# Moving the indexer's dots behind their rope, turning the attention outputs and moving the pool tiles in a two-layer decoder step

## What is computed

```python
dots = jnp.einsum('bqhd,bld->bqhl', qi, ki) * (IDX_DIM ** -0.5)
s = jnp.einsum('bqhl,bqh->bql', jax.nn.relu(dots), wi) * (N_IDX_HEADS ** -0.5)
_, sel = lax.top_k(s, topk)
p = jax.nn.softmax(where(valid, q @ k_sel, -inf)); o = p @ v_sel
out = jnp.einsum('btgc,gcd->btgd', window_mean(xp) - xp, w_pool) * pool_scale
```

## Time and profile before

| | |
|---|---|
| time, median of 3 runs | 1589.93 us (1585.71 to 1590.79) |
| profiled execution: its time, its span | 1585.85 us, 1584.1 us |
| busy: PE, DVE, ACT, POOL | 1435.0, 803.7, 432.3, 184.1 us |
| mean granted clock of TensorE | 0.932 |
| layer 1: third indexer query tile begins | 852.0 us |
| page products end | 907.0 us |
| unit loop begins | 989.5 us |
| output projection begins | 1106.5 us |
| layer 0: the same four | 75.2, 132.0, 214.6, 331.7 us |

### The profile page before, as it was taken

How to read it: one execution, slowest core, us unless ns; L and a number is a source line. 1 busy time by engine, 2 the same in 40 slices (tenths; PEclk the granted TensorE clock), 3 DMA queues, 4 the chain that set the end, 5 groups by cost and what they waited for, 6 DMA issues and landing times. The chain is left out here.

```text
span 1584.1 us, 25392 instructions
## 1 busy us (share of the span) xinstructions
PE 1435.0 (91%) x9676; PEld 1239.6 (78%) x9676; DVE 803.7 (51%) x1752; ACT 432.3 (27%) x761; POOL 184.1 (12%) x200
## 2 busy tenths in 40 slices
PE   4999957998899999999988988599979999999995
PEld 2765643687899999999957547356969999999995
DVE  1127777434665656712142486863366565665221
ACT  3111113534322222422131120254342222224220
POOL 1000354002100000000040005430030000000002
PEclk8999976898999999999979999587989999999997
DMA  8870112002122222222159402020212222222321
GB/s 322 176 103 27 34 36 77 5 28 80 67 93 89 85 91 93 86 97 88 69 215 172 87 1 70 1 81 1 80 41 94 93 87 87 91 103 74 111 76 54
DMA packets 46316, 133.17 MB, mean 84 GB/s; under 512 B 6319, under 2 KB 25615, under 8 KB 38911
## 3 DMA queue, kind: packets, MB, share of 16 engines
q1 hardware_dynamic: 43423, 119.52, 25.2%
q0 software_dynamic: 2816, 12.62, 2.3%
HBM read 119.94 MB, written 12.82 MB: 84 GB/s over the span
## 5 line engine op out<-in xcount | busy, mean ns | idle before, releaser
L779 PE MATMUL ps<-moR_r,W_r 128*128 128x260 f32 x1408 | 285.4, 284 | 0.0
L779 PEld LDWEIGHTS ps<-moR_r,W_r 128*128 128x128 f32 x1408 | 218.1, 190 | 0.0
L779 PE MATMUL ps<-hT_r,QZC_r 128*128 128x260 f32 x896 | 183.4, 286 | 0.0
L779 PE MATMUL ps<-moR_r,QZC_r 128*128 128x260 f32 x704 | 146.5, 289 | 12.3 <-DVE hT_r L1822 12.1
L779 PE MATMUL ps<-moR_r,SQ_r 128*128 128x260 f32 x704 | 142.1, 283 | 0.0
L779 PEld LDWEIGHTS ps<-hT_r,QZC_r 128*128 128x128 f32 x896 | 141.3, 193 | 0.0
L779 PE MATMUL ps<-hT_r,SQ_r 128*128 128x260 f32 x704 | 140.6, 281 | 0.0
L766 PE MATMUL ps<-hT,W 128*128 128x260 f32 x576 | 132.8, 388 | 0.0
L779 PEld LDWEIGHTS ps<-moR_r,QZC_r 128*128 128x128 f32 x704 | 110.6, 192 | 16.0 <-issue 8.6
L766 PEld LDWEIGHTS ps<-hT,W 128*128 128x128 f32 x576 | 109.4, 192 | 17.1 <-issue 0.6
L1864 DVE TENSOR_TENSOR SEL<-ps,rstd 128x520 f32<-128x520 f32 x44 | 30.8, 700 | 154.3 <-PE ps L779 149.4
(11 more groups left out here) (318 smaller groups left out, 2728.0 us busy)
## 6 DMA issues: line engine op xcount, KB each, us to landing
W<-in_w_gates SPq DMA_DIRECT2D x44, 512.0 KB, 3.2
W<-in_w_vals SPq DMA_DIRECT2D x44, 512.0 KB, 3.2
W<-in_w_downs SPq DMA_DIRECT2D x16, 1408.0 KB, 6.0
W<-in_w_pairs SPq DMA_DIRECT2D x12, 1024.0 KB, 7.5
pages_by_slot<-moR SPq DMA_DIRECT2D x8, 1024.0 KB, 5.4
yR<-pages_by_slot SPq DMA_DIRECT2D x16, 512.0 KB, 17.9
W<-in_w_outs SPq DMA_DIRECT2D x8, 1024.0 KB, 4.9
W<-in_w_kv SPq DMA_DIRECT2D x2, 1312.0 KB, 10.3
```

The source lines that it names most:

```text
L779: last = mm(ps[:, 2 * (g % 2) + f, 0:HT], w(k), x(k)[:, f * HT:(f + 1) * HT], start=(k == 0 and n == 0), stop=(k == nk - 1 and n == 2))
```

## The change

Dots are ordered by head pair, then token tile, and stand between the k steps of the tiles that follow the pair's rope (six dots a tile, in the last two indexer query tiles and XP 0 and 1). The search's counts stand between the k steps of XP 2, 3 and the query tiles; ranks follow every other step. Probabilities stay unscaled; `values` takes them as the stationary side (128 columns) and the value rows as the moving side (64), so that queries lie on partitions, and once a token tile VectorE scales its 8 units by the reciprocal sums and TensorE turns the result back. Pool tiles go to unit 24 behind `sample_max`, with their scaling on VectorE; the sample's steps move to earlier units.

```diff
-SCORED = 10
-ROPES = {16: (4,), 18: (5,), 19: (6,)}
+DOTS = [(t, h) for j in range(4) for t in (1, 2, 3) for h in (2 * j, 2 * j + 1)]
+ROPES = {12: (4,), 15: (5,), 17: (6,)}
...
+        ON = SQ[:, 3, 0:SEQ]
-        att = sb("att", [P, 4, 4])
+        att = sb("att", [P, 4])
+        sums = sb("sums", [P, 2, N_HEADS])
...
-                    if extras and k % 4 == 3:
+                    if extras and k in at:
                         extras.pop(0)()
...
+                def dot(d):
+                    def go():
+                        t, h = DOTS[d]
+                        if d == 0:
+                            pe.wait_ge(*kt_ev(l, 4))
+                        if d % 6 == 0:
+                            wait_alone(pe, *rope_done(l, d // 6 + 1))
+                        if d >= 2:
+                            wait_alone(pe, *dot_relu(l, d - 1))
+                        rows = slice(64 * (h % 2), 64 * (h % 2) + 64)
+                        mm(ps[:, 4 + d % 2, 0:P * (t + 1)], qiT[rows, h // 2, t * P:(t + 1) * P],
+                           kiT[rows, 0:P * (t + 1)], start=True, stop=True).then_inc(dot_mm.sem, 1)
+                    return go
...
-                    tile8(QI_T + j, 1 + j // 2, j % 2)
+                    tile8(QI_T + j, 1 + j // 2, j % 2, extras=dots, at=range(2, KD) if j >= 2 else ())
...
+                tile8(XP_T, 3, 0, extras=dots, at=range(2, KD))
                 pe.wait_ge(*rope_done(l, 4))
...
+                tile8(XP_T + 1, 3, 1, extras=dots, at=range(1, KD - 1))
...
+                steps = [scores_by_page] + [count(s) for s in range(COUNTS)] + [pick_a, pick_b, pick_c]
+                page_products()
+                arrived(l, 4)
+                for j in (2, 3):
+                    pe.wait_ge(*evac(l, XP_T + j - 1))
+                    tile8(XP_T + j, 4, j % 2, extras=steps, at=(1, 4, 7) if j == 2 else (1, 3, 5, 7))
...
-                    tile8(Q_T + j, 5 + j // 2, j % 2, extras=counts)
+                    tile8(Q_T + j, 5 + j // 2, j % 2, extras=steps, at=(1, 4, 7))
...
-                    wait_alone(pe, *list_ev(l, 1))
-                    pe.wait_ge(*o_ev(l, 1))
+                    wait_alone(pe, *ss_ready(l, 1))
+                    pe.wait_ge(*qs_ev(l, 2))
+                    pe.wait_ge(*o_ev(l, 2))
...
-                picks = {6: pick_d, 14: pool_tiles, 26: sample_scores, 28: scores_by_row, 33: sample_probs_turned,
-                         34: sample_values}
-                picks.update({21 + q: (lambda q=q: keys_turned(q)) for q in range(4)})
+                def outputs_turned(t):
+                    wait_alone(pe, *o_normed(l, t + 1))
+                    for j in range(4):
+                        last = turn(ps[:, 6 + t % 2, j * P:(j + 1) * P], ON[:, j * P:(j + 1) * P], ident)
+                    last.then_inc(o_turned.sem, 1)
+                picks = {5: pick_d, 21: sample_scores, 23: scores_by_row, 24: pool_tiles, 28: sample_probs_turned,
+                         30: sample_values}
+                picks.update({17 + q: (lambda q=q: keys_turned(q)) for q in range(4)})
+                turned = {8 * t + 12: t for t in range(NT - 1)}
...
-                    pe.wait_ge(*prob_ready(l, i + 1))
+                    pe.wait_ge(*exp_done(l, i + 1))
...
-                        last = mm(ps[64 * n:64 * n + 64, 6 + t % 2, j * P:(j + 1) * P],
-                                  NAT[:, kt, 200 + 64 * n:264 + 64 * n], ART[:, i % 2, kt * P:(kt + 1) * P],
-                                  start=(kt == 0), stop=(kt == t))
+                        last = mm(ps[:, 6 + t % 2, 64 * p:64 * p + 64], ART[:, i % 2, kt * P:(kt + 1) * P],
+                                  NAT[:, kt, 200 + 64 * n:264 + 64 * n], start=(kt == 0), stop=(kt == t))
...
+                    elif steps:
+                        steps.pop(0)()
+                    if i in turned:
+                        outputs_turned(turned[i])
...
+                outputs_turned(NT - 1)
...
+                for ropes, first in (((0,), 0), ((1,), 6), ((2, 3), 12)):
+                    for j in ropes:
+                        rope(j)
+                    for d in range(first, first + 6):
+                        add_dots(d)
...
                 for n, step in enumerate(steps):
                     step()
+                    rank(n % 2)
                     for j in ROPES.get(n, ()):
                         rope(j)
-                rank(4)
-                rope(7)
+                    if n == 18:
+                        rank(3)
+                        rope(7)
...
-                picks = {0: slots, 1: hot_high, 2: hot_low, 3: hot_rows, 9: pick_e, 30: sample_max, 32: sample_probs}
+                picks = {0: slots, 1: hot_high, 2: hot_low, 3: hot_rows, 7: pick_e, 26: sample_probs}
...
-                def normalised(i):
-                    n = P * (1 + i // N_HEADS)
-                    dve.wait_ge(*exp_done(l, i + 1))
-                    then_wait(nc.vector.reciprocal(att[:, i % 4, 2:3], att[:, i % 4, 1:2]))
-                    ts(ARP[i % 4][:, 0:n], ARP[i % 4][:, 0:n], att[:, i % 4, 2:3], None, ALU.mult
-                       ).then_inc(prob_ready.sem, 1)
+                def outputs_normed(t):
+                    dve.wait_ge(*pv_mm(l, N_HEADS * (t + 1)))
+                    if t:
+                        dve.wait_ge(*o_turned(l, t))
+                    nc.vector.reciprocal(sums[:, t % 2, :], sums[:, t % 2, :]).then_inc(o_recip.sem, 1)
+                    wait_alone(dve, *o_recip(l, t + 1))
+                    tt(ON.rearrange("p (h d) -> p h d", h=N_HEADS),
+                       ps[:, 6 + t % 2, :].rearrange("p (h d) -> p h d", h=N_HEADS),
+                       sums[:, t % 2, :].unsqueeze(2).broadcast_to([P, N_HEADS, HD]), ALU.mult).then_inc(o_normed.sem, 1)
+                def pool_out():
+                    for g in range(4):
+                        dve.wait_ge(*tile_done(l, PM_T + g + 1))
+                        ts(hT[:, 4 + g, 0:SEQ], ps[:, 3 + 4 * (g % 2), :], vecs[:, l, 32 + g:33 + g], None, ALU.mult
+                           ).then_inc(pm_ev.sem, 1)
...
+                for i in range(UNITS):
+                    if 3 <= i < 24:
+                        rank(-(-len(ranks) // (24 - i)))
...
+                    masked(i)
+                    if i == 24:
+                        sample_max()
+                        pool_out()
...
+                    if i in (11, 19, 27):
+                        outputs_normed(i // 8 - 1)
...
+                outputs_normed(NT - 1)
```

More of the change, by code:

```diff
@@ L331, in count_bank @@
         def count_bank(s):
-            return (6 if s < 23 - SCORED else 4) + s % 2
+            return 4 + s % 2
         def halves(ap):
@@ L758, in arrived, with product @@
                 pe.wait_ge(*w_in_slot[c % 2](l, 16 * dmas_before(c)))
-            def product(g, lhsT, rhs, nk, extras=None, before=None):
+            def product(g, lhsT, rhs, nk, extras=None, at=(), before=None):
                 for k in range(nk):
@@ L821, in partner @@
                     last.then_inc(rot_mm.sem, 1)
+                def dot(d):
[11 more added lines that the diff above has]
+                    return go
+                dots = [dot(d) for d in range(24)]
                 for j in range(4):
@@ L1219, in layer, with relu @@
                 copy(kT[:, SEQ:TOK], ps[:, 7, 8:8 + NB]).then_inc(kt_ev.sem, 1)
-                q_copy(2, QI_T + 2)
-                q_copy(3, QI_T + 3)
+                def relu(d):
+                    t, h = DOTS[d]
+                    n = P * (t + 1)
+                    act.wait_ge(*dot_mm(l, d + 1))
+                    if d >= 4:
+                        act.wait_ge(*dot_acc(l, d - 3))
+                    nc.scalar.activation(RB[:, d % 4, 0:n], ps[:, 4 + d % 2, 0:n], ACT.Relu).then_inc(dot_relu.sem, 1)
+                for j in range(2):
+                    for d in range(6 * j, 6 * j + 6):
+                        relu(d)
+                    q_copy(2 + j, QI_T + 2 + j)
+                for d in range(12, 18):
+                    relu(d)
                 def xp_copy(j):
@@ L1524, in rope @@
                     tt(dst, TS[:, :], QC[:, j % 2, :], ALU.add).then_inc(rope_done.sem, 1)
-                for j in range(4):
-                    rope(j)
                 def best(t, r):
@@ L1582, in layer @@
                 ts(spread, const("spread"), wcol[:, 8:9], None, ALU.mult).then_inc(w_spread.sem, 2)
+                for d in range(18, 24):
+                    add_dots(d)
                 dve.wait_ge(*sdot_mm(l, 1))
@@ L1587, in layer @@
                 nc.vector.tensor_reduce(snew[:, :], sdot[:, :], AX.X, ALU.add).then_inc(snew_ready.sem, 1)
-                for d in range(8):
-                    add_dots(d)
                 for r in range(TOPK_P // 8):
@@ L1758, in masked @@
                     nc.vector.tensor_tensor_reduce(ARS[:, i % 2, 0:n], ps[:, i % 3, 0:n], out, -1.0, -TAKEN,
[L1759 to L1766 removed]
```

(8 more changed lines are left out.)

159 lines of the change are left out of this document (67 added, 92 removed).

## The result

The changed kernel takes **1625.97 us** (median of 4 runs, 1621.16 to 1629.73), the kernel before beside it 1590.36: a ratio of 1.023 (95% interval 1.019 to 1.027), 35.6 us slower. The prediction had 12.6 us slower and a range that ended at 1616. The side was right; the size was a third of what came.

What follows compares the result with a forecast made beforehand. VectorE was taken to bound only the top-k ranking beside attention units 0 to 14, with TensorE busy elsewhere. Terms 18.8 - 21.5 - 11.9 + 20.9 gave +6.3 us a layer, +12.6 for two: 1602.5 us, range 1580 to 1616.

Steps and rivals of the forecast that it cites:

- A: Third indexer query tile to end of page products, dots moved in behind the rope: +18.8 us a layer.
- B: End of page products to start of unit loop, search beside XP 2, 3 and query tiles: -21.5 us a layer.
- so waits of some 2 us: Search stage before the unit loop: TensorE waits some 2 us for VectorE's search steps of 2.50 us each.
- C: Start of unit loop to unit 16's scores, with fewer ranks and no normalisations: -11.9 us a layer.
- some 8 is only that the pool tiles have left: Units 0 to 15: some 8 of the 11.9 us gained comes from pool tiles leaving, having stood in VectorE's shadow.
- D: Unit 16's scores to the output projection: 8.7 - 0.8 + 1.8 + 1.2 + 4 + 6 = +20.9 us a layer.
- gather wait: Near unit 17: TensorE arrives near 1038.7, the last gather lands at 1042.7: +4 us a layer.
- wait for the maximum: Unit 24: TensorE idles 2.6 us for the mask and sample_max before the pool tiles, part of their +8.7 us.
- the clock term: From unit 16: TensorE at 1.2 GHz until about unit 20, +6 us a layer, ends 0 and 11.
- Rival 2: Value products at half price, 0.13 us each: 0 us a layer, 1590 us; chance 0.12.
- Rival 3: Low clock up to the pool tiles and again at the end: +12.3 us a layer, 1614.5 us; chance 0.20.
- Rival 1: Clock holds at 2.4 GHz from unit 16 through the sample's scores: -4.2 us a layer, 1581.5 us; chance 0.20.

Runs made afterwards that it cites:

- x11_steps_back: The changed kernel with pool tiles at unit 14 (ScalarE scaling) and the sample's steps in their old units; moved dots and new outputs stay: 1599.47 us, ratio 1.006.
- x13_keys_early: The kernel before with only the turns of the gathered keys moved from unit 21 to unit 17: 1610.65 us, ratio 1.015.
- x10_early: The kernel before with only the sample's steps moved to the changed kernel's units, four to six earlier; pool tiles stay at 14: 1625.61 us, ratio 1.024.
- x7_newvalues: The kernel before with the new outputs alone (64 value columns moving, probabilities unscaled, outputs scaled and turned a token tile at a time): 1597.41 us, ratio 1.003.
- x1_pool16: The changed kernel with pool tiles at unit 16 in place of 24, scaled by ScalarE again: 1616.98 us, ratio 1.019.
- x3_narrow: The changed kernel with 32 added products of 8 columns in unit 17, ahead of the wait for gathered keys: 1649.15 us, ratio 1.037.
- x2_wide: The changed kernel with four added products of 128x512 in unit 17, ahead of the wait for gathered keys, results unread: 1614.53 us, ratio 1.018.

## Why the prediction was wrong, step by step

- **A** (+18.8 predicted; +16.4 and +18.2): right. Dots and their k steps take what the rows of before said.
- **B** (-21.5; -17.8 and -16.3): the step that failed is "so waits of some 2 us". TensorE waits 4.7 and 6.0 us for the search. Its own work is 54.6 and 54.8 us busy (2 more than the 52.5 of the sum), and the waits behind the last query tile, 5.7 and 5.4 us, are under the 6.5 given. VectorE's 2.50 us a step held only where no rank (some 3.0 us with one) and no GpSimd operation stood in it.
- **C** (-11.9; -11.7 and -11.8): right as a sum, but not in the split "some 8 is only that the pool tiles have left": with them at unit 14 again, x11_steps_back has C at 51.7, so their leaving is worth 4.5.
- **D** (+20.9; +27.1 and +29.5): gather wait (3.0 and 4.2), wait for the maximum (2.7), end (1.2) and values (0.235 us a product at 2.4 GHz; predicted 0.24) came as priced. Rival 2 is out. (The estimate of 0.21 us worked out from the Trainium skill, TensorE: Matmul & The Clock Gate, section LDWEIGHTS, is 0.025 below the measured product.) The step that failed, and the larger of the two, is the clock term, +6 with "The drop behind sample_scores costs about what it did (0)". The +6 and the gather's 4 were about right for what they cover: x13_keys_early, which has just these two in the kernel before, with its old value products, measured 8.8 and 11.5. The return came in layer 0 at unit 21, 15.8 us behind the first key turn (forecast: 13.3, unit 20), just ahead of the sample's scores, and in layer 1 not before them. But the drop behind the scores was priced at nothing though the change moved it among other units and gave these other products. It lasted until the pool tiles ended it, 14.7 us and about half of their own 6.3 (0.73) in layer 0 and all of 1079 to 1106 in layer 1. The drop behind the sample's values lasted to the end in layer 0 (0.50) and for most of what was left in layer 1 (0.63).
- **Rival 3** (low clock up to the pool tiles and again at the end, +12.3 a layer, chance 0.20) is what happened, up to its price: with B's 3.7 and 5.2 us on top its 1614.5 would have been 1623.4. Its argument against, "it needs a low stretch longer than any in the trace beside full work", was no argument: no stretch of before had these products in it. Rival 1 is out: units 16 to 23 never ran at 1.00, but for the scores of unit 21 in layer 0.

## What to carry to other kernels

When a step is moved, price again what follows it in its new place, the clock above all: a drop that lasted 12 us behind the same 16 products lasted 29 behind them five units earlier (x10_early), and 44, up to the end of the loop, when the value products that follow took 64 moving and 128 stationary columns in place of 128 and 64 (x7_newvalues). A busy TensorE is not always a TensorE at 2.4 GHz (61.4 of 62.6 us busy at 0.50 in x1_pool16); in a stage where it is the bound, look up in the trace what TensorE does behind each drop, and whether the change puts other work there. And move a consumer of a gather forward only as far as the gather lands: here, in x13_keys_early, a wait of 2.6 us came with 9 to 12 us more in the stage.

## What was not expected of the hardware

- TensorE stayed at 1.2 GHz for 62.6 us while busy in 61.4 of them (x1_pool16), and for 13.7 us of back-to-back 8-column products (x3_narrow), and rose within 6.4 us of four products of 512 columns (x2_wide). The Trainium skill (TensorE: Matmul & The Clock Gate, section What's actually happening) has the clock follow how busy the engine has been; by these runs the busy time that a profile shows does not decide it alone.
- Four products a layer whose results nobody reads made a kernel 9 to 11 us faster (x2_wide).
- A VectorE operation of 0.22 us took 2.09 when a GpSimd addition of 3.69 us was under way, and ended with it within 0.02 us.
